# Queries and keys produced already transposed in the latent up-projection and in the memory attentions, their RMS roots applied later

## The reference, cut to what matters

```python
def mla_mixer(h, cos, sin, w_dkv, g_q, g_kv, w_uq, w_ukv, w_o):
    lat = h @ w_dkv
    c_q = rmsnorm_2(lat[..., :384], g_q)
    c_kv = rmsnorm_2(lat[..., 384:640], g_kv)
    k_pe = lat[..., 640:][:, :, None, :]
    q = (c_q @ w_uq).reshape(B, S, 8, 128 + 64)
    kv = (c_kv @ w_ukv).reshape(B, S, 8, 128 + 128)
    q_pe, k_pe = apply_rope(q[..., 128:], cos, sin), apply_rope(k_pe, cos, sin)
    ...causal softmax attention of 8 heads, then @ w_o

def mem_cross_attn(h, m, w_q, w_kv, w_o):
    q = (h @ w_q).reshape(B, S, 4, 128)
    kv = (m @ w_kv).reshape(B, 256, 2, 4, 128)
    s = jnp.einsum('bqhd,bmhd->bhqm', q, kv[:, :, 0]) * 128 ** -0.5
    o = jnp.einsum('bhqm,bmhd->bqhd', softmax(s), kv[:, :, 1])
    return o.reshape(B, S, 512) @ w_o
```

## Time and profile before

| | |
|---|---|
| median of 3 runs | 1272.52 us (1272.42 to 1272.82) |
| the profiled execution: its time / its span | 1272.93 us / 1271.0 us |
| TensorE busy | 1257.9 us, 99% |
| VectorE, ScalarE busy | 756.7 us (60%), 656.1 us (52%) |
| granted TensorE clock, mean | 0.998 |

### The profile page before, as it was taken

How to read it: one execution, slowest core, us unless ns; L and a number is a source line. 1 busy time by engine, 2 the same in 40 slices (tenths; PEclk the granted TensorE clock), 3 DMA queues, 4 the chain that set the end, 5 groups by cost and what they waited for, 6 DMA issues and landing times.

```text
span 1271.0 us, 16754 instructions
## 1 busy us (share of the span) xinstructions
PE 1257.9 (99%) x6734; PEld 1081.4 (85%) x6734; DVE 756.7 (60%) x1056; ACT 656.1 (52%) x846; POOL 21.1 (2%) x25
## 2 busy tenths in 40 slices
PE   9999999999999999999999999999999999999997
PEld 7888888888888888889888799989888887999896
DVE  6555448788675554447765675454553655754553
ACT  6454437464455444436954564443465745643433
POOL 0000000001000000000000000000000000000001
PEclk9999999999999999999999999999999999999999
DMA  8855546554533655544633265554565332665540
GB/s 291 291 178 197 185 151 209 217 182 138 177 133 125 242 180 195 179 135 169 240 125 116 83 240 192 199 177 135 185 232 184 115 108 91 226 216 176 195 133 34
DMA packets 39213, 221.71 MB, mean 174 GB/s; under 512 B 4486, under 2 KB 5142, under 8 KB 23649
## 3 DMA queue, kind: packets, MB, share of 16 engines
q1 hardware_dynamic: 36672, 214.20, 48.8%
q0 software_dynamic: 1024, 4.22, 1.0%
q10 hardware_dynamic: 1440, 2.22, 0.6%
HBM read 219.56 MB, written 1.07 MB: 174 GB/s over the span
## 4 chain that ended last, share of the span: by engine, by line
PE 93%; DVE 3%; ACT 2%; issue 1%; DMA 1%; POOL 0%; SPq 0%; DVEq 0%; ACTq 0%
PE ps L403 23%; PE ps L405 23%; PE ps L404 23%; PE ps L612 5%; PE ps L611 5%; PE ps L610 5%; PE ps L1424 2%; PE ps L1449 2%; PE ps L437 1%; DVE wlo L368 1%; PE ps L984 1%; PE ps L1436 1%; PE ps L643 1%; DMA w_raw<-ffn_first 1%; ACT whi L360 0%
## 5 line engine op out<-in xcount | busy, mean ns | idle before, releaser
L368 DVE TENSOR_TENSOR wlo<-w_raw,whi 128x2048 fp32r<-128x2048 f32 (+4 forms) x244 | 468.5, 1927 | 379.2 <-ACT whi L360 379.0
L360 ACT ACTIVATE whi<-w_raw 128x2048 fp32r<-128x2048 f32 (+4 forms) x244 | 393.3, 1618 | 407.3 <-PE ps L405 304.9
L403 PE MATMUL ps<-whi,xt_h 128*128 128x512 f32 (+3 forms) x784 | 308.8, 394 | 1.5 <-DVE nat L790 0.8
L405 PE MATMUL ps<-whi,xt_l 128*128 128x512 f32 (+3 forms) x784 | 302.5, 386 | 0.0
L404 PE MATMUL ps<-wlo,xt_h 128*128 128x512 f32 (+3 forms) x784 | 301.8, 385 | 0.0
L403 PE MATMUL ps<-whi,ot_h 128*128 128x512 f32 x594 | 235.1, 396 | 0.0
L405 PE MATMUL ps<-whi,ot_l 128*128 128x512 f32 x594 | 231.7, 390 | 0.0
L404 PE MATMUL ps<-wlo,ot_h 128*128 128x512 f32 x594 | 231.4, 390 | 0.0
L403 PEld LDWEIGHTS ps<-whi,xt_h 128*128 128x128 f32 x784 | 147.3, 188 | 32.7 <-issue 4.8
L405 PEld LDWEIGHTS ps<-whi,xt_l 128*128 128x128 f32 x784 | 147.1, 188 | 29.6
L404 PEld LDWEIGHTS ps<-wlo,xt_h 128*128 128x128 f32 x784 | 147.4, 188 | 27.3
(11 more groups left out here) (227 smaller groups left out, 875.7 us busy)
## 6 DMA issues: line engine op xcount, KB each, us to landing
w_raw<-ffn_mid SPq DMA_DIRECT2D x80, 768.0 KB, 4.3
w_raw<-mlp_mid SPq DMA_DIRECT2D x56, 1024.0 KB, 5.0
w_raw<-w_qkv SPq DMA_DIRECT2D x12, 1024.0 KB, 5.0
w_raw<-w_sb_qkv SPq DMA_DIRECT2D x12, 1024.0 KB, 4.9
w_raw<-w_xkv SPq DMA_DIRECT2D x8, 1024.0 KB, 4.9
w_raw<-ffn_first SPq DMA_DIRECT2D x8, 512.0 KB, 4.4
w_raw<-w_gate_b SPq DMA_DIRECT2D x4, 1024.0 KB, 4.9
w_raw<-w_gate_a SPq DMA_DIRECT2D x4, 1024.0 KB, 5.0
```

The lines of the kernel that those rows point to most:

```text
L360: nc.scalar.activation(whi[:, s, 0:tiles * width], w_raw[:, s, 0:tiles * width], ACT.Copy).then_inc(w_hi, 1)
L368: nc.vector.tensor_tensor(wlo[:, s, 0:tiles * width], w_raw[:, s, 0:tiles * width], whi[:, s, 0:tiles * width].bitcast(F32), ALU.subtract) ...
L403: nc.tensor.matmul(acc, hi, whi[:, s, c], start=start, stop=False)
L405: return nc.tensor.matmul(acc, lo, whi[:, s, c], start=False, stop=stop)
```

## The change

1. **`LatentUp` replaces `Project` for the up-projection.** The order is now pe, q, q, k, k, v, v. pe and v stay as before. For q and k the weights are stationary and 256 positions move (`pair`: two heads into the two halves of a bank), so the result lands transposed and ScalarE (q, L1344) or VectorE (k, L1414) copies it straight to `qt`/`kt`. The 32 transposes of q and k go.
2. **The roots.** q's root goes to the exponent: `scale=-root` (`minus`) in the exponential and one multiplication of the maxima in each group (`log_vector`). k's root is needed along the moving axis: VectorE makes two diagonals (L1407), TensorE multiplies them by a block of -1 (L1320), ScalarE copies the row (L1372, `spread_in`), and `take_k` multiplies by it.
3. **Memory attention.** Queries are made the same way, one head to a bank; the root goes to the exponent. Groups are now head pairs (both tiles of heads 0-1, then of heads 2-3). Head 3's projection stands between the scores of groups 0, 1 and 2, 3. All four groups are divided on VectorE. The output of a head pair is split by one pair of instructions of 512 columns (L2409, L2414).

```diff
+        class LatentUp:
+            def pair(self, pe, n, p, k0, tiles):
+                take_chunk(pe, n)
+                for j in range(2):
+                    for k in range(tiles):
+                        at = k * TW + (2 * p + j) % 4 * P
+                        cols, acc = slice(at, at + P), bankA[p % 2][:, j * S:(j + 1) * S]
+                        nc.tensor.matmul(acc, whi[:, slot_of(n), cols], ot_h[:, k0 + k], start=k == 0, stop=False)
+                        nc.tensor.matmul(acc, wlo[:, slot_of(n), cols], ot_h[:, k0 + k], start=False, stop=False)
+                        last = nc.tensor.matmul(acc, whi[:, slot_of(n), cols], ot_l[:, k0 + k], start=False,
...
+            def tensor(self, pe):
...
+                for t in range(NT):
+                    pe.wait_ge(before.evac, t + 1)
+                    self.rows(pe, self.pe, t, 0, 3)
+                before.turn(pe, before.units[-1])
+                for p in range(4):
+                    pe.wait_ge(self.evac, p + 1)
+                    self.pair(pe, self.q[p // 2], p, 0, 3)
+                self.aside.tensor(pe)
...
+                pe.wait_ge(self.diagonal, 1)
+                for t in range(NT):
+                    last = nc.tensor.matmul(bankT[0][:, t * P:(t + 1) * P], const[:, C_ONES:C_ONES + P],
+                                            self.diagonals[:, t * P:(t + 1) * P], start=True, stop=True)
+                last.then_inc(self.spread, 1)
+                for p in range(4):
+                    if p < 2:
+                        pe.wait_ge(self.evac, 5 + p)
+                    else:
+                        pe.wait_ge(self.k_taken, p - 1)
+                    self.pair(pe, self.k[p // 2], p, 3, 2)
+                self.turn(pe)
...
+            def scalar(self, act):
...
+                self.aside.scalar(act)
+                act.wait_ge(self.spread, 1)
+                nc.scalar.activation(self.factors, bankT[0][:, 0:S], ACT.Copy).then_inc(self.spread_in, 1)
+                next_hi(act, self.k[0])
+                self.take_turned(act)
+                act.wait_ge(self.before.rooted, 2)
+                self.take_v(act, 0)
+                next_hi(act, self.k[1])
+                self.take_v(act, 1)
+                next_hi(act, self.v[0])
+                next_hi(act, self.v[1])
...
+            def take_k(self, dve, p):
+                dve.wait_ge(self.spread_in, 1)
+                dve.wait_ge(self.full, 7 + p)
...
+            def vector(self, dve):
+                self.factor(dve)
+                self.rotate(dve, 0)
+                self.rotate(dve, 1)
+                next_lo(dve, self.pe)
+                next_lo(dve, self.q[0])
+                next_lo(dve, self.q[1])
+                self.aside.vector(dve)
+                self.take_k(dve, 0)
+                self.take_k(dve, 1)
+                next_lo(dve, self.k[0])
+                self.take_k(dve, 2)
+                self.take_k(dve, 3)
+                next_lo(dve, self.k[1])
+                next_lo(dve, self.v[0])
+                next_lo(dve, self.v[1])
...
             def tensor(self, pe):
...
+                self.query(pe, [0, 1, 2], [6, 7])
                 pe.wait_ge(*self.keys_ready)
-                pe.wait_ge(self.q.taken, 1)
+                pe.wait_ge(cross_taken, NXH * i + 2)
                 att.score(pe, 0)
-                self.q.turn_tile(pe, self.unit, 1)
                 att.score(pe, 1)
-                pe.wait_ge(self.q.taken, 2)
+                used(self.query(pe, [3], [0, 1, 2, 3]), self.q0)
+                self.query(pe, [3], [4, 5, 6, 7])
+                att.turn(pe, 0)
+                pe.wait_ge(cross_taken, NXH * (i + 1))
                 att.score(pe, 2)
                 att.score(pe, 3)
-                att.turn(pe, 0)
+                att.turn(pe, 1)
                 pe.wait_ge(*self.values_ready)
-                att.turn(pe, 1)
                 att.value(pe, 0)
+                att.value(pe, 1)
                 att.turn(pe, 2)
-                att.value(pe, 1)
                 att.turn(pe, 3)
                 att.value(pe, 2)
                 att.value(pe, 3)
```

More of the change, by code:

```diff
@@ L1508, in exp_scalar @@
                     last = nc.scalar.activation(rows, self.bank(g)[:, cols] if self.bare else rows, ACT.Exp,
-                                                bias=nmax[:, c:c + 1], scale=1.0 if self.bare else -1.0,
+                                                bias=nmax[:, c:c + 1], scale=head["row"] if self.bare else head.get("minus", -1.0),
                                                 accum_out=rsum[:, c:c + 1])
@@ L1558, in log_vector @@
                         accum_out=nmax[:, c:c + 1])
+                heads = self.groups[g]
+                if "row" in heads[0]:
+                    own(dve, dve_own, last)
+                    c, n = heads[0]["col"], len(heads)
+                    last = nc.vector.tensor_scalar(nmax[:, c:c + n], nmax[:, c:c + n], heads[0]["row"], None, ALU.mult)
                 last.then_inc(self.logits, 1)
@@ L2132, in gpsimd @@
                 pass
-        class CrossAttention:
[L2139 to L2156, removed]
+        cross_q = sem("cross_q")
@@ new lines, in build, with __init__, q_bank, query @@
+        cross_taken = sem("cross_taken")
+        cross_out_hi = sem("cross_out_hi")
+        cross_out_lo = sem("cross_out_lo")
+        cross_full = sem("cross_full")
+        class CrossAttention:
+            def __init__(self, i, fills, groups, like=None):
+                self.i, self.cross, self.mlp = i, f"cross{i}", f"mlp{i}"
+                self.att = Attend(f"mem{i}", groups, [], [], turned=True, bare=True, like=like and like.att)
+                self.keys_ready, self.values_ready = fills[0].ready, fills[1].ready
+                self.q0, self.n0 = AT[f"xq{i}"], AT[f"xo{i}"]
+                self.full0 = NB * NT * i
+                ends[self.q0 + 1] = (cross_q, NXH * (i + 1))
+                ends[self.n0], ends[self.n0 + 1] = (cross_full, self.full0 + NT), (cross_full, self.full0 + NB * NT)
+            def q_bank(self, head):
+                return (bankA + bankT)[head][:, 0:S]
+            def query(self, pe, heads, ks):
+                for head in heads:
+                    for k in ks:
+                        if head == 0 and k % 2 == 0:
+                            xt_ready(pe, self.cross, k)
+                        cols = slice(k % 4 * TW + head * P, k % 4 * TW + (head + 1) * P)
+                        n = slot_of(self.q0 + k // 4)
+                        nc.tensor.matmul(self.q_bank(head), whi[:, n, cols], xt_h[:, k], start=k == 0, stop=False)
+                        nc.tensor.matmul(self.q_bank(head), wlo[:, n, cols], xt_h[:, k], start=False, stop=False)
+                        last = nc.tensor.matmul(self.q_bank(head), whi[:, n, cols], xt_l[:, k], start=False,
+                                                stop=k == KC - 1)
+                    if ks[-1] == KC - 1:
+                        last.then_inc(cross_q, 1)
@@ L2208, in tensor @@
[L2208 to L2216, removed]
-                nc.scalar.activation(qt[:, 0:4, t * P:(t + 1) * P], bankT[t].rearrange("p (c s) -> p c s", c=4),
-                                     ACT.Copy, scale=self.unit.scale).then_inc(self.q.taken, 1)
+                pe.wait_ge(cross_out_lo, 2 * i + 1)
@@ L2220, in scalar @@
             def scalar(self, act):
[L2221 removed]
+                att = self.att
                 nc.scalar.preload_act_table_set("natural_log_exp_and_others")
[L2223 to L2230 removed]
@@ L2587, in mla_groups @@
                         group.append(dict(
-                            at=i * keys, width=keys, tile=t, head=hd,
+                            at=i * keys, width=keys, tile=t, head=hd, row=qrow(t), minus=mla_up.minus(0, t),
                             bias=const[:, C_CAUSAL + S - keys:C_CAUSAL + S],
```

280 lines of the change are left out of this document (186 added, 94 removed).

## The result

The changed kernel takes 1276.41 us (median of 8 runs, 1275.13 to 1277.28), the kernel before 1272.84 us beside it (1272.42 to 1273.09): ratio 1.0027, 95% interval 1.0019 to 1.0036. It is slower by 3.6 us, 0.27%. Forecast were 1273.3 us, with a range up to 1276.0. The profiled execution of after took 1275.13 us, the lowest of its runs.

The account below looks back on a forecast made before the run. TensorE, busy 99% of the span, and pauses forced on it bound the kernel. +3.4 us to the first transposition of probabilities, -2.6 us in memory attentions: +0.8 us, so 1273.3 us; range 1270.9 to 1276.0.

Parts of the forecast that it names:

- The clock falls in the first pause: Up-projection, third key pair: TensorE resumes at half speed, 1.9 us lost once, 1275.2 us; chance 0.2 of slower, 0.15 of less.
- TensorE's work: Up-projection: more but narrower matmuls and a spread row, 32 transposes fewer; together -2.4 us.
- waits of before that go: Up-projection: waits present in the kernel before, counted as 0.5 us saved if no new pauses come.
- First pause: Up-projection, third key pair: TensorE waits 4.1 us until VectorE has copied the first pair out of its bank.
- Second pause: Latent attention, first transposition of probabilities: TensorE waits 2.2 us behind VectorE's remainders, mask and division.
- the scale from a column: Latent attention's exponentials: a column instead of a constant costs nothing, at most 0.1 us on each of four.
- No extra in groups 1 to 5: Latent attention: the root's multiplication, 0.2 us per group, costs nothing there, 1.0 us if there is no slack.
- Memory attentions: Both memory attentions: less work and no GpSimd wait, partly eaten by new pauses; -1.3 us each, -2.6 us together.
- they gain nothing: Memory attentions: VectorE, with all four divisions, becomes what TensorE waits for; 1275.9 us, chance 0.05.
- no pause comes: Up-projection: key copies fall earlier than laid out, so 1267.0 us; chance 0.12 for anything below 1270.0.
- Sum: Whole kernel: +3.4 us less 2.6 us for the memory attentions gives +0.8 us.
- the test named as decisive: Profile sign: granted clock of 0.50 after 620 us, or L1414 ending before two key pairs, would prove the forecast wrong.

Follow-up runs that it names:

- the constant scale: Against the changed kernel, the latent attention's exponentials take the constant -1 as scale and the maximum without the root; 1275.55 us.
- the second pause taken away: Against the changed kernel, VectorE masks the first score group ahead of the last 2048-column remainder and divides it right behind; 1273.51 us.
- the first filled half: Against the changed kernel, 15 unused 256-column matmuls at the third key pair and 19 before the first transposition of probabilities; 1274.93 us.
- both filled: Against the changed kernel, 30 unused 256-column matmuls at the third key pair and 19 before the first transposition of probabilities; 1274.05 us.
- the first pause taken away: Against the changed kernel, spread row ahead of memory-row transposes, and VectorE copies keys earlier with two remainders ahead, memory rows behind; 1271.20 us.

## Why the prediction was wrong

The step that failed is in the sum: it has no term for the clock. "The clock falls in the first pause" stood only among the rivals, with 0.35 in all and 1.9 us once, because TensorE is busy on both sides of the pause. It happened: in every trace with the first pause the clock is halved around its end. The lowered clock is worth 2.4 us in the median: 1.4 us behind the first pause, where the traces show 1.5 to 1.6 us, and 0.9 us that the times put behind the second and no trace shows. Even the rival's own time, 1275.2 us, was too low, for it stood on a sum that was short by the smaller terms below.

The Trainium skill (TensorE: Matmul & The Clock Gate, HAM oscillation) describes the clock being halved in waits for DMA of about 3 to 5 us between bursts of matmuls. For the first pause, 3.9 us, the trace agrees (0.57 over 4 us). The prediction read it as speaking for both pauses; the second, 2.6 us, is shorter than the waits described there, and no trace of it shows a fall.

- *TensorE's work, -2.4 us*: with the waits of before that go (0.5 us by the prediction) 2.9 us were forecast for the up-projection; measured are 2.6 us with no pause in it. 0.3 us too much.
- *First pause, 4.1 us*: measured 3.9 us, at the place and by the instruction named.
- *Second pause, 2.2 us*: measured 2.6 us. The missing 0.4 us is the scale from a column, which I costed at nothing, at most 0.1 us on each of four exponentials: it is 0.09 us on each and stands in the chain whole. With the constant scale the wait is 2.05 us instead of 2.42.
- *No extra in groups 1 to 5*: right, no wait is charged there.
- *Memory attentions, -1.3 us each*: 1.2 and 1.1 us by the trace. The rivals that they gain nothing, or that no pause comes, fell.
- *Sum*: predicted +0.8 us. With 2.4 for the clock, 0.4 for the exponentials, 0.3 less from the memory attentions, 0.3 less saved in the up-projection and 0.2 less of first pause it is +4.0; measured were 3.6 us, and the 0.4 us between them are within the scatter. By the trace TensorE stands 40.19 - 34.97 = 5.2 us behind its former place at the first transposition of probabilities, where 3.4 were forecast, and 1.5 of the missing 1.8 us are the clock.

The first memory attention's MLP was to come about 2 us later than before; it came 735.15 + 0.66 - 731.78 = 4.0 us later. And the test named as decisive, a clock of 0.50 after 620 us, is what the trace shows.

## What to carry to other kernels

A new pause of TensorE of 2 us and more is to be priced with a part for the clock on top, and in the sum, not only among the rivals. Here a fall cost 1.5 to 1.6 us in four traces and about 2.5 us in one, whether the wait was 3.9 or 2.0 us; it came in all four traces with the wait of 3.9 us, and in some only of those with about 2 us. When a copy out of PSUM goes from one engine to another, look first at what already stands in the new engine's queue: the same change is 3.6 us slower in one order of these queues and 5.1 us faster in another. Filling a pause with useless matmuls is a cheap way to measure what the pause costs in clock.

## What the runs showed that was not expected

- When the clock falls differs between executions with the same pause of 3.9 us: 1.5 us after work resumes in after (pause to 622.72, slow from 624.26), at about the same moment as work resumes with the second pause taken away (first matmul at 623.15, clock 0.79 over 623.0 to 623.5), and inside the pause with the constant scale. It is low for 3.4 us in the first two and for 6.9 us in the last.
- TensorE's clock of 1.00 survives the shorter waits of before (1.2 us at most), and falls behind waits near 2 us in some executions and not in others: a fall behind 2.0 us (the first filled half) and behind 2.07 and 1.93 us for the input at the start (both filled, constant scale), none behind 2.2 and 2.4 us (the second pause) and 2.29 us (the start with the first pause taken away).
- A scale read from a column makes an exponential of 128 columns 0.48 us long instead of 0.39. The Trainium skill (ScalarE: Activation LUTs, What ACT_TABLE_LOAD costs) gives about 93 ns for each operand of this kind; the traces agree, and the sum should have had it four times.
- With the memory part alone changed, the last store needs 0.9 us more to its end; its size and its place in the program are the same as in before.
